# Seven steps of 512 instead of four of 896 in an expert layer, with weights laid out part by part

## The reference

```python
def swiglu(t, w_gate, w_up, w_down):
    return (jax.nn.silu(t @ w_gate) * (t @ w_up)) @ w_down

def moe_swiglu(h, router_w, w_gate, w_up, w_down):     # t: 256 x 1024, D_FF_2 = 3584
    logits = t @ router_w; top_v, top_i = lax.top_k(logits, 2); top_p = softmax(top_v)
    for e in range(8):
        out = out + gates[:, e:e + 1] * swiglu(t, w_gate[e], w_up[e], w_down[e])
```

## Time and profile before

| what | us |
|---|---|
| median of 3 runs | 2924.63 (2921.05 to 2924.83) |
| span of the profiled execution | 2916.6 |
| the eight experts in it, first expert matmul to the end of the last down | 1875 to 2886 |
| PE, PEld, DVE, ACT, POOL busy, share of the span | 97, 91, 67, 56, 16% |
| chain of work that ended last | PE 82%, DVE 9%, ACT 6%, issue 2%, DMA 1% |
| mean granted TensorE clock | 0.976 |

### The profile page before, as it was taken

The page is one execution under the profiler, slowest core; times in us unless marked ns, Lnnn a source line. Parts: engine busy times, 40 slices in busy tenths (PEclk is TensorE's granted clock), DMA queues, the critical chain, the costliest instruction groups (busy, mean ns, idle before and its releaser), DMA issues.

```text
span 2916.6 us, 42979 instructions
## 1 busy us (share of the span) xinstructions
PE 2840.0 (97%) x18565; PEld 2640.4 (91%) x18578; DVE 1941.0 (67%) x1967; ACT 1623.0 (56%) x1787; POOL 462.5 (16%) x215
## 2 busy tenths in 40 slices
PE   8999999999999999999999999999999999999997
PEld 7999999999999999989899988899898989889886
DVE  5677647766676567735467624487877878777774
ACT  4555446554555465522477512476767667677763
POOL 1000000001000000000000000133333333333332
PEclk9999999999999999989999989899999999999998
DMA  7645456726445477551688731399999999999993
GB/s 231 172 145 174 145 194 235 265 81 180 152 136 181 136 260 246 166 156 59 204 293 293 233 106 53 130 371 337 369 335 350 351 351 358 336 368 333 349 356 126
DMA packets 355543, 679.12 MB, mean 233 GB/s; under 512 B 17265, under 2 KB 237713, under 8 KB 355217
## 3 DMA queue, kind: packets, MB, share of 16 engines
q1 hardware_dynamic: 339712, 616.49, 60.7%
q0 software_dynamic: 15632, 59.80, 6.4%
HBM read 675.19 MB, written 4.69 MB: 233 GB/s over the span
## 4 chain that ended last, share of the span: by engine, by line
PE 82%; DVE 9%; ACT 6%; issue 2%; DMA 1%; POOL 0%; SPq 0%; DVEq 0%; ACTq 0%
PE bank L568 79%; DVE w_lo L1364 4%; ACT w_hi L1953 3%; DVE ring_tail L1323 1%; PE bank L1189 1%; ACT ring_tail L2005 1%; PE bank L664 1%; PE bank L689 1%; DVE ring_tail L1325 1%; DVE gates L1377 1%; DMA ring_head<-in_w_in 0%; DVE ring_low L1293 0%; PE bank L715 0%; PE bank L640 0%; DMA ring_head<-in_w_mix_out 0%
## 5 line engine op out<-in xcount | busy, mean ns | idle before, releaser
L1859 DVE TENSOR_TENSOR ew_lo<-ring_head,ew_hi 128x1792 fp32r<-128x1792 f32 (+1 forms) x288 | 680.5, 2395 | 199.6 <-ACT ew_hi L2271 199.6
L2271 ACT CAST ew_hi<-ring_head 128x1792 fp32r<-128x1792 f32 (+2 forms) x384 | 647.1, 1694 | 274.7 <-PE bank L568 274.7
L549 POOL TENSOR_TENSOR ew_lo<-ring_head,ew_hi 128x1792 fp32r<-128x1792 f32 (+1 forms) x96 | 388.7, 4049 | 859.3 <-ACT ew_hi L2271 859.3
L568 PE MATMUL bank<-xs_hi,ring_low 128*128 128x256 f32 x1984 | 388.9, 282 | 0.0
L568 PE MATMUL bank<-x_hi,w_hi 128*128 128x256 f32 x1152 | 323.4, 287 | 15.3 <-DVE w_lo L1364 14.9
L1364 DVE TENSOR_TENSOR w_lo<-ring_head,w_hi 128x2048 fp32r<-128x2048 f32 x108 | 247.5, 2292 | 126.2 <-ACT w_hi L1953 126.2
L568 PE MATMUL bank<-x_hi,w_lo 128*128 128x256 f32 x1152 | 318.4, 283 | 0.0
L568 PE MATMUL bank<-x_lo,w_hi 128*128 128x256 f32 x1152 | 318.4, 283 | 0.0
L568 PEld LDWEIGHTS bank<-xs_hi,ring_low 128*128 128x128 f32 x1984 | 313.3, 188 | 0.7
L568 PE MATMUL bank<-ew_hi,xe_hi 128*128 128x448 f32 x1024 | 295.1, 370 | 4.4 <-DVE ew_lo L1859 4.4
L568 PE MATMUL bank<-ew_lo,xe_hi 128*128 128x448 f32 x1024 | 291.6, 366 | 0.0
(11 more groups left out here) (391 smaller groups left out, 5799.4 us busy)
## 6 DMA issues: line engine op xcount, KB each, us to landing
ring_head<-in_moe_w_gate SPq DMA_DIRECT2D x128, 896.0 KB, 6.6
ring_head<-in_moe_w_up SPq DMA_DIRECT2D x128, 896.0 KB, 6.8
ring_head<-in_moe_w_down SPq DMA_DIRECT2D x96, 1024.0 KB, 7.0
ring_head<-in_w_in SPq DMA_DIRECT2D x76, 1024.0 KB, 5.6
ring_tail<-in_ada_w POOLq DMA_DIRECT2D x48, 1024.0 KB, 7.3
ring_head<-in_ffn_w_in SPq DMA_DIRECT2D x44, 1024.0 KB, 6.6
ring_head<-in_ffn_w_out SPq DMA_DIRECT2D x22, 1024.0 KB, 8.3
ring_head<-in_xa_kv SPq DMA_DIRECT2D x16, 1024.0 KB, 5.4
```

What stands on the lines that cost most here:

```text
L549: pool.tensor_tensor(ew_lo[:, h, 0:n], ring(c % 6)[:, 0:n], ew_hi[:, h, 0:n].bitcast(F32), ALU.subtract).then_inc(w_used[c % 6], 1)
L568: ins = nc.tensor.matmul(out, lhsT, rhs, start=start, stop=stop, **kw)
L1859: v.tensor_tensor(ew_lo[:, h, 0:n], ring(c % 6)[:, 0:n], ew_hi[:, h, 0:n].bitcast(F32), ALU.subtract).then_inc(w_used[c % 6], 1)
L2271: a.copy(ew_hi[:, c % DEPTH_HI, 0:n], ring(c % 6)[:, 0:n]).then_inc(f.count(part_hi), 1)
```

## The change

Experts go in seven steps of 512 ff columns. Gate and up take two parts each in a step (four blocks of 128 rows x 512 columns), down takes two. Every part now has 2048 elements per partition (1 MB) and 12 matmuls of 512 columns, and an expert has 42 parts. A gate or up product writes a single PSUM bank. Because 42 is no multiple of 4, the slot of a part in `ew_hi`/`ew_lo` is counted on through the experts, and POOL takes the parts of slot 3: parts 3, 7, 11 ... of an even expert (counted from 0), parts 1, 5, 9 ... of an odd one. The places of `form` and `finish` in the lists are renumbered. The experts' weights are rearranged by numpy before the launch, so that a part is 8 KB contiguous per partition in memory.

```diff
-EC = 896
+EC = 512
 ETILES = EC // P
-EHALF = EC // 2
+WK = CH // EC
...
-PARTS = [(kind, s, i) for kind, s in EXPERT_PARTS for i in range(4)]
-FIRST = {(kind, s): 4 * n for n, (kind, s) in enumerate(EXPERT_PARTS)}
+PARTS = [(kind, s, i) for kind, s in EXPERT_PARTS for i in range(2)]
+FIRST = {(kind, s): 2 * n for n, (kind, s) in enumerate(EXPERT_PARTS)}
...
-                                load(part, c % 6, ffn_loaded)
+                                w = {"gate": wg, "up": wu, "down": wd}[kind]
+                                load(tiles(w[e, 2 * step + i], 2 if kind == "down" else WK), c % 6, ffn_loaded)
...
-                        h = c % DEPTH_HI
+                        h = (e * len(PARTS) + c) % DEPTH_HI
                         f.bump(part_hi)
-                        if c % 4 == 3:
+                        if h == 3:
                             pool.wait_ge(part_hi, f.now(part_hi))
-                            pool.tensor_tensor(ew_lo[:, h, 0:n], ring(c % 6)[:, 0:n], ew_hi[:, h, 0:n].bitcast(F32),
+                            pool.tensor_tensor(ew_lo[:, h, :], ring(c % 6), ew_hi[:, h, :].bitcast(F32),
...
-                        for i in range(4):
-                            hi, lo = part(FIRST[kind, step] + i, 2, EC)
-                            for k in range(2):
-                                t = 2 * i + k
+                        for i in range(2):
+                            hi, lo = part(e, FIRST[kind, step] + i, WK)
+                            for k in range(WK):
+                                t = WK * i + k
                                 for x, w, last in ((xe_hi, hi, False), (xe_hi, lo, False), (xe_lo, hi, True)):
-                                    for n in range(2):
-                                        mm(bank[b + n][:, 0:EHALF], x[:, t, :], w[:, k, n * EHALF:(n + 1) * EHALF],
-                                           t == 0 and w is hi and x is xe_hi, t == KD - 1 and last,
-                                           part_done if last and (k, n) == (1, 1) else None)
+                                    mm(bank[b][:, :], x[:, t, :], w[:, k, :], t == 0 and w is hi and x is xe_hi, t == KD - 1 and last,
+                                       part_done if last and k == WK - 1 else None)
...
-                                    if c == FIRST["up", s] + 7:
-                                        form(base + FIRST["up", s] + 4)
-                                low(c)
-                                if (kind, i) == ("up", 3) and step:
+                                    if c == FIRST["up", s] + 5:
+                                        form(base + FIRST["up", s] + 2)
+                                low(e, c)
+                                if (kind, i) == ("down", 0) and step < STEPS - 1:
                                     finish()
...
-                                high(c, base + c + 1 - DEPTH_HI)
+                                high(e, c, base + c + 1 - DEPTH_HI)
...
-                                    if c == FIRST["gate", s] + 7:
+                                    if c == FIRST["gate", s] + 5:
...
+def parts_of_widening(w):
+
+    w = np.asarray(w)[0].reshape(EXPERTS, 2, WK, P, STEPS, EC)
+    return w.transpose(0, 4, 1, 3, 2, 5).reshape(EXPERTS, 2 * STEPS, P, CH)
+
+
+def parts_of_down(w):
+
+    w = np.asarray(w)[0].reshape(EXPERTS, 2 * STEPS, 2, P, D)
+    return w.transpose(0, 1, 3, 2, 4).reshape(EXPERTS, 2 * STEPS, P, CH)
```

More of the change, by code:

```diff
@@ L266, in program @@
         esilu, eact = flat[:, 0:EC], flat[:, 1024:1024 + EC]
-        both = tiles(banks[:, 6:8, :].rearrange("p b c -> p (b c)")[:, 0:EC], ETILES)
+        both = tiles(bank[6], ETILES)
         back = kb[:, 2, :]
@@ L542, in experts @@
                 for e in range(EXPERTS):
-                    for c, (kind, step, i) in enumerate(PARTS):
-                        n = 2 * EC if kind != "down" else D * (min(2 * i + 2, ETILES) - 2 * i)
-                        h = c % DEPTH_HI
+                    for c in range(len(PARTS)):
+                        h = (e * len(PARTS) + c) % DEPTH_HI
                         f.bump(part_hi)
-                        if c % 4 == 3:
+                        if h == 3:
                             pool.wait_ge(part_hi, f.now(part_hi))
-                            pool.tensor_tensor(ew_lo[:, h, 0:n], ring(c % 6)[:, 0:n], ew_hi[:, h, 0:n].bitcast(F32),
+                            pool.tensor_tensor(ew_lo[:, h, :], ring(c % 6), ew_hi[:, h, :].bitcast(F32),
                                                ALU.subtract).then_inc(w_used[c % 6], 1)
@@ L1190, in turn, with down @@
                         ins.then_inc(f.count(turned), 1)
-                    def down(step):
+                    def down(e, step):
                         pe.wait_ge(eact_ready, f.next(eact_ready))
-                        for i in range(4):
-                            tops = range(2 * i, min(2 * i + 2, ETILES))
-                            hi, lo = part(FIRST["down", step] + i, len(tops), D)
+                        for i in range(2):
+                            tops = range(2 * i, 2 * i + 2)
+                            hi, lo = part(e, FIRST["down", step] + i, 2)
                             for t in tops:
@@ L1236, in experts @@
                                 pe.wait_ge(gate_silu, f.next(gate_silu))
-                                widen("gate", step, 0)
+                                widen(e, "gate", step, 0)
                                 if e and step == 1:
@@ L1240, in experts @@
                                 turn()
-                                widen("up", step, 2)
+                                widen(e, "up", step, 2)
                                 if e and step == 1:
@@ L1244, in experts @@
                                     f.bump(result_free, 4)
-                                down(step - 1)
+                                down(e, step - 1)
                             pe.wait_ge(gate_silu, f.next(gate_silu))
@@ L1848, in _, with low @@
                     v.tensor_scalar(crowded[:, :], crowd[:, 0:1], float(P), None, ALU.is_gt).then_inc(f.count(crowd_ready), 1)
[L1850 to L1855, removed]
+                    def low(e, c):
+                        h = (e * len(PARTS) + c) % DEPTH_HI
+                        if h == 3:
                             f.bump(part_hi)
@@ L1865, in form @@
                         dve.wait_ge(gate_silu, f.next(gate_silu))
-                        v.tensor_tensor(tiles(eact, 2), tiles(esilu, 2), banks[:, 2:4, 0:EHALF], ALU.mult).then_inc(f.count(turn_ready), 1)
+                        v.tensor_tensor(eact, esilu, bank[2], ALU.mult).then_inc(f.count(turn_ready), 1)
                     def finish():
@@ L2262, in _, with high @@
                         take(4 + q, htok[:, q // 2, 512 * (q % 2):512 * (q % 2) + 512], bank[4 + q][:, :])
-                    def high(c, done):
-                        kind, step, i = PARTS[c]
-                        n = 2 * EC if kind != "down" else D * (min(2 * i + 2, ETILES) - 2 * i)
+                    def high(e, c, done):
                         if done > 0:
@@ L2270, in high @@
                         eng.wait_ge(ffn_loaded[c % 6], f.next(ffn_loaded[c % 6], 16))
-                        a.copy(ew_hi[:, c % DEPTH_HI, 0:n], ring(c % 6)[:, 0:n]).then_inc(f.count(part_hi), 1)
+                        a.copy(ew_hi[:, (e * len(PARTS) + c) % DEPTH_HI, :], ring(c % 6)).then_inc(f.count(part_hi), 1)
                     def form():
-                        a.activation(tiles(esilu, 2), banks[:, 0:2, 0:EHALF], ACT.Silu).then_inc(f.count(gate_silu), 1)
+                        a.activation(esilu, bank[0], ACT.Silu).then_inc(f.count(gate_silu), 1)
                     def finish():
@@ L2370, in layout @@
     arrays["memT"] = np.ascontiguousarray(np.asarray(i["mem"])[0].T)
+    for n in ("moe_w_gate_2", "moe_w_up_2"):
+        arrays[n] = parts_of_widening(i[n])
+    arrays["moe_w_down_2"] = parts_of_down(i["moe_w_down_2"])
     arrays["const"] = constants()
```

24 lines of the change are left out of this document (10 added, 14 removed).

## The result

The changed kernel takes 2929.2 us against 2917.4 for the kernel before, both medians of 20 runs; the ratio is 1.0038, with a 95% interval of 1.0029 to 1.0047. One of the 20 runs of the kernel before took 4652.7 us and counts in no ratio. By the ratio the change is 11 us slower (8 to 14), where the forecast said 8. The profiled execution has a span of 2927.1 us, 10.4 more than the one of before.

The account below looks back on a forecast made before the run. PE was taken as the bound, with DVE and POOL subtractions 95% full and hidden behind it. Terms -13.3 + 0.5 - 1.5 - 2.9 + 15 + 9.9 gave +7.7 us, so 2932.3 us; range 2913 to 2945.

Parts of the forecast that it names:

- gate and up matmuls: PE in the experts: 2688 matmuls of 512 columns replace 3072 of 448, saving 13.3 us of fixed cost.
- last turn's wait: End of the last expert: PE's wait of 2.98 us for DVE's split shrinks to 1.5 us, so -1.5 us.
- clock behind it: After the last turn: the shorter rest leaves PE's clock at 2.4 GHz instead of granted 0.50, so -2.9 us.
- common line: DVE's and POOL's SBUF subtractions never run at once; 99% full after the change, costing 15 us inside eight experts.
- second part at odd seams: Before four odd experts POOL's part 1 waits for DVE, making PE 1.8 us later each time: 7.1 us.
- first part at seams: At seven seams between experts DVE's first subtraction makes PE 0.4 us late, 2.8 us in all.
- rival 2: PE's 512-column matmuls in one bank cost in proportion (231.7 ns), saving nothing; 2935 us, chance 0.09.
- POOL's time: POOL's subtraction of 2048 elements takes 4.5 us; 0.1 us more or less moves the total by up to 8 us.
- Rival 1: Inside experts, DVE's and POOL's subtractions still fit in PE's time and only the seam costs; -7.3 us, 2917.3 us, chance 0.27.
- Rival 3: PE's rests at the seams bring the clock to 1.2 GHz, 12 us on top, 2944 us; chance 0.08.
- Rival 4: Weight loads don't become long runs or the DMA rate limits; 5 to 10 us on top, 2940 us; chance 0.05.
- Rival 5: POOL overlaps better inside experts and at seams, so all costs vanish; -17 us, 2907.5 us; chance 0.06.

Follow-up runs that it names:

- e3: Changed kernel with every weight subtraction on DVE, none on POOL; ratio to the kernel before 0.9960, expert stretch 997.7 us.
- e5: Changed kernel with all weight subtractions on DVE and the next expert's first two parts cast before the last turn's copy; ratio 0.9946, stretch 994.5 us.
- e11: Changed kernel with POOL subtracting one part in eight instead of one in four; ratio to the kernel before 0.9974, stretch 1003.0 us.
- e6: Kernel before with POOL's subtraction always over 2048 elements whatever the part's size; one run, 3014.8 us, stretch 1100.4 us.
- e2: Changed kernel with the weights in their original memory layout; ratio to the kernel before 1.0047, stretch 1022.1 us.
- e1: Kernel before with only the weights' memory layout changed, each part contiguous per partition; ratio 0.9995, stretch 1009.3 us.
- e9: Kernel before with all weight subtractions on DVE, its last-turn split ahead of the subtraction of the expert's last part; ratio 0.9999, stretch 1008.7 us.
- e7: Kernel before with every weight subtraction on DVE, none on POOL; ratio 1.0034, stretch 1018.2 us.

## Why the prediction was right

The sign, the place and the kind of the loss were right, and the size nearly. Term by term, for the expert stretch:

| term | forecast | measured | from |
|---|---|---|---|
| gate and up matmuls | -13.3 | -13.1 | 2688 x 226.8 ns, less 622.7 |
| last turn's wait | -1.5 | -1.8 | idle of 2.98, now 1.2 |
| clock behind it | -2.9 | -2.9 | no stretch of 0.50, but see below |
| common line, with the second part at odd seams | +22.1 | +24.1 | after less e3 |
| first part at seams | +2.8 | +3.2 | e3 less e5 |
| not assigned | | +0.7 | |
| sum | +7.2 | +10.2 | |

**The matmuls.** The distance in one bank is 226.8 ns, as in two; rival 2 is out. By the rule of the Trainium skill that the prediction weighed (TensorE: Matmul & The Clock Gate, Wait — 56ns, not 53.3ns?: 2.5 ns over the columns) it would be 215.8 ns, an estimate from that page. The trace doesn't agree: an expert matmul of 512 has 13.5 ns over them, in the changed kernel and in all its variants.

**POOL's time.** I worked out 4.5 us for 2048 elements from two other sizes, and it is 4.48 and 4.50. The Trainium skill has 4497 and 2293 ns for the two engines, for an addition of this size (GPSIMD Engine Reference, 3.1 Elementwise — side-by-side cycle accounting). This case's trace agrees, 4.48 to 4.50 and 2.29. Neither figure holds beside the other engine: the means in the changed kernel are 5991 and 3158 ns.

**The line.** The waits came at the parts that I had stepped to: the twenty-fourth part of an even expert 0.58 late where I had 0.6, and 1.5 at the second part of odd experts where I had 1.8. The term that was too small is the one inside experts: 15 forecast, 17.3 measured (24.1 less 6.8, four gaps of 1.53 at the odd seams with 0.15 of restart behind each). My own 2.2 and 1.7 us for an even and an odd expert make 15.6, not 15. Against e3, part by part, they came out unequal: the even experts lose 3.4 to 3.5 us each, only the very first 2.0, and the odd ones 1.2 to 1.3. So the even ones were put too low and the odd ones too high, and the sum hides part of it.

I charged the splits and products, but not what else stands in DVE's queue: the four selections of an expert, which also wait for POOL (below), and the eight additions of the finished expert's result, 0.47 us each. Nor did I charge the restart: behind a late part PE loses another 0.1 to 0.2. The first expert has the selections but neither additions nor a seam before it, and it loses the least of the even ones, so the selections alone don't make the surplus of the others. How it divides among selections, additions and the seam no run shows.

**Rival 1**, that the line still fits at 99%, is refuted by e3 and e11: the limit was where I had put it, and not the latency of a POOL part. But e11 shows how near the two are: a line with 11% of room (29.8 of 33.5 us) leaves 5.3 us, most of it at the seams. **Rival 3** did not occur in the changed kernel, where the longest rest between experts is 1.4 us; e6 shows that it does occur with longer rests. **Rival 4** is out: e2 and the absence of waits for landings. **Rival 5** was wrong as a prediction and right as a price: e5 is what the change gives when the line is out of the way, 17.0 us less in the stretch, as I had it, the clock of the next paragraph included.

**The step that was right by luck** is the clock at the last turn. I let a rest of 2.98 us bring the fall and one of 1.5 avoid it. The same rest is followed by 0.50 in before and by 1.00 in e1 and e9, and both of these have a stretch of 1009.3 or 1008.7 instead of 1011.5. So 2.2 to 2.9 us of the difference between the two profiled executions most likely belong to that execution of before, not to the change. Against a stretch of 1009 the changed kernel loses 13 us, in the upper part of the timed interval of 8 to 14. What decides whether a rest of 3 us is followed by the slow level stays open. The rest of 4.1 us in e7 was; of 13 rests of 2.5 to 2.6 us in e6 ten were and three were not; the rests of 1.6 and less in the changed kernel and its variants never. There is luck in the last line of the forecast, too: 2932.3 us is only 3 above the measured 2929.2, because the base of three runs, 2924.6, lay 7 above the median of twenty, while the difference was put 4 too low.

## What to carry to other kernels

Before work is shared between DVE and POOL, look whether they ever run at once: take one instruction of each that overlap in the time line, and see whether the later one's duration is its own or its own plus the other's rest. If they exclude each other, count them as one engine, and give the work to the faster one alone; here a part costs the line 2.2 us on DVE and 4.5 on POOL. A hidden resource at 95% of the bound is the first place to look when a change makes every piece of work a little larger, and an operation that PE waits for goes ahead of preparatory work in a queue, all the more where that work can be blocked.

## What was not expected of the hardware

DVE's comparison that builds the weighing matrix has one tensor operand in SBUF, and the rows show it blocked too. Of the changed kernel, then of e3 (count | busy us, mean ns):

```profile
L1873 DVE TENSOR_SCALAR kb<-const,picks 128x128 f32<-128x128 f32 x16 | 22.0, 1417 | 0.0
```

```profile
L1863 DVE TENSOR_SCALAR kb<-const,picks 128x128 f32<-128x128 f32 x16 | 4.8, 340 | 0.0
```

It takes 1417 ns on average beside POOL and 340 without. The products and splits with an operand in PSUM keep their time in both (674 and 680 ns for the product). That 128 columns of comparison can wait for 2048 elements of POOL is 17 us of DVE's time in the experts, which I had not counted.

The second surprise is that 8 KB runs in place of 2 and 4 KB change nothing for a load stream at 0.92 to 0.95 of the DMA engines' time, since all landings were in time already.
